# Last block of a hybrid mLSTM / chunk-MLP step: sample statistics moved, gate scans split, block end by token tile

## The chip, the cores and the metric

The kernel runs on one core of a Trainium2 chip. The metric is the device time of one execution in microseconds (us), as a median of several runs. Names of engines: PE is the matrix engine, DVE the vector engine, ACT the scalar engine, POOL the GpSimd engine, SP the queue that issues most loads.

## What is computed

One decoder layer for two groups with the same weights: a prompt of 2048 tokens and a group of 8 samples of one token each, which start from a stored state. Model width is 1024; there are 4 mLSTM heads and 4 chunk-MLP heads of width 128; the SwiGLU mixer has 2816 hidden columns. Everything is float32. The core of the reference, shortened:

```python
h = rmsnorm(x, g_norm1) * (1 + sc1) + sh1
q, k, vm, o, ig, fg, u, vs = split_cols(h @ w_in, IN_SIZES)
h_ml, C, n, m = mlstm_chunkwise(q, k, vm, i_pre, f_pre, C0, n0, m0)
h_ml = rmsnorm(h_ml, g_mlstm_head) * sigmoid(o)
vs = layernorm(gelu(vs), ln_v_g, ln_v_b)
h_cm = chunk_spatial_gate(gelu(u), vs, w_s, b_s)
x = x + gt1 * (concat([h_ml, h_cm]) @ w_out)
h2 = rmsnorm(x, g_norm2) * (1 + sc2) + sh2
a, bb = split(h2 @ w_gate_up)
x = x + gt2 * ((silu(a) * bb) @ w_down)
y = rmsnorm(x, g_final)
```

In `mlstm_chunkwise` the gates of a chunk of 128 tokens become b, the running sum of log_sigmoid(f), and a running maximum m_t; both scale the chunk's attention matrix and the state that goes to the next chunk. For one sample token these are a few numbers per head, and the state update is C_new = w_i C + w_g v k^T, with h = C_new q / den.

## The kernel before, in words

The prompt goes through in four blocks of 512 tokens (`NBLK`, `TT` = 4 token tiles of 128 each). The first block also works out the modulation, blocks 1 and 2 are a loop, and the last block also carries the samples and ends the program. Each engine has its own instruction list in program order; they meet at semaphores.

**Slabs.** Weights come in slabs of 512 KB. For slab s of a block, SP loads `raw` (two buffers), ACT rounds it into `w_hi` (`split_hi`, L842), DVE takes the difference into `w_lo` (`split_lo`, L1311), and PE makes three products per 128 rows (L1798 to L1800): hi times lo, lo times hi, hi times hi. `w_hi` and `w_lo` have two buffers as well, so slab s+2 can be split only when PE is done with slab s, and SP may load slab s only when slab s-2 has its low part.

**The order of the first part.** `PRE` and `MIX` are lists of steps that all engines go through. An integer s is the product of slab s of `w_in` on PE; at the same step ACT moves slab s out of its bank and splits slab s+2, and DVE makes the low part of slab s+2. Between them stand the prompt's gates: "R1" (`gate_sum`, L1329 to L1334), "R2" (`gate_log` on ACT: exp, then ln), "R3" (`gate_scans` on DVE, L1341 to L1357), "R4" (`gate_weights` on ACT) and "COL". R3 is four running sums (L1345), a difference, and then four times a running maximum (L1352) followed by one addition (L1354), with each waiting for the one before; two row operations end it, and they release `row_m`. SP waits for `row_m` ahead of slab 10's load.

**The samples** are put between these steps in the last block by the table `SAMPLES`, which PE, ACT and DVE all follow at the integer steps (DVE after its low part):

```python
SAMPLES = {2: ("SG",), 3: ("SW",), 4: ("SD",), 5: ("SC", "SV"), 6: ("C0",), 7: ("C1", "C2"), ...
```

SG is the samples' gates and two dot products, SW the stabiliser, SD the denominators, SC three copies out of PE's banks with one product that releases `wv_set` (L1260), SV the statistics of the samples' layernorm (six DVE steps, L1264 to L1269, after a gelu that ACT makes in SD, L811), and C0 to C7 update one sample's state each (three DVE steps, L1303 to L1306). On POOL `samples_state` (L633 to L640: three small products, then eight scalings of the stored states, after `wv_set`) comes first and `samples_mixing` (L583, L648 to L659: seven steps on 8 rows, after SV) second. `samples_mixing` needs the row `lnrow`, which SP loads at slab 8 (L469).

**The end of the last block.** The last slab's products fill four banks, a token tile each. For each tile DVE multiplies by the gate and adds to `x1` (`down_tiles`, L1477, L1479), ACT sums the squares of the tile's right half (L759; the left half's squares were summed during the slabs before). After the four tiles DVE copies the samples' product out (`s_ev`, L1628), PE turns it (`sample_turn`, L1832), DVE adds it (`sample_residual`), PE sums the squares (L1859), DVE takes the means (L1081, L1086), POOL the roots (L583), and DVE scales whole rows of `x1` by root and final gain (L1641, 1024 wide). SP stores each tile when its row is done (L559). The samples' result is turned by PE (L2162), moved out by ACT and DVE (L1033, L1659) and stored by ACT.

## Time and profile before

| | |
|---|---|
| median of 3 runs | 2534.2 us (2533.69 to 2534.28) |
| the profiled execution | 2534.6 us, of which the span of instructions is 2533.1 us |
| busy share of the span | PE 97%, DVE 47%, ACT 33%, POOL 7% |
| mean granted clock of PE | 0.989 of full speed |
| DMA | 280.13 MB, mean 111 GB/s |

All times inside the program are counted from the start of the span. A row of a timeline has the start, the duration, the engine, the line of the kernel and the operation with what it writes and reads; in brackets stands how long the engine sat idle before it and what ended that. The last block's first slab product begins at about 1844 us; the end of its last slab product is near 2514.8 us.

### The profile page before, as it was taken

The numbers are of one execution on the slowest core, as the hardware profiler recorded it, in microseconds if no ns is written. First come the engines' busy times: TensorE is split into PE (matmuls) and PEld (weight loads), VectorE is DVE, ScalarE is ACT, GpSimd is POOL, SyncE is SP. The second block draws the span as 40 slices with busy tenths as digits, with TensorE's granted clock in tenths as the row PEclk, the third lists the DMA queues.
The fourth block names the chain that finished last, engine by engine and source line by source line (L and its number), as shares of the span: only waits on it lengthen the run. The fifth ranks groups of instructions, "written<-read, shape, count | busy, mean of one in ns | idle before, by whom it ended". The sixth has DMA issues, their size and how long they took to land.

```text
span 2533.1 us, 32802 instructions
## 1 busy us (share of the span) xinstructions
PE 2454.7 (97%) x12328; PEld 1982.8 (78%) x12328; DVE 1202.8 (47%) x1741; ACT 846.2 (33%) x1149; POOL 182.8 (7%) x147
## 2 busy tenths in 40 slices
PE   5999999999999999999999999999988999999997
PEld 3688877888888888888888878888876877777775
DVE  4648545434347554444346654444367853333323
ACT  2343322233244243333244243333253323323211
POOL 0022000000003000000003100000033200000000
PEclk8999999999999999999999999999999999999998
DMA  7732365332342243332342333333354222222222
GB/s 274 260 100 80 116 191 173 109 94 96 114 115 70 89 125 91 99 100 89 100 137 71 98 112 95 98 93 97 99 185 134 79 67 77 81 83 83 87 88 76
DMA packets 361043, 280.13 MB, mean 111 GB/s; under 512 B 11288, under 2 KB 302652, under 8 KB 360919
## 3 DMA queue, kind: packets, MB, share of 16 engines
q1 hardware_dynamic: 333012, 228.91, 30.2%
q10 hardware_dynamic: 23956, 34.81, 4.0%
q0 software_dynamic: 3968, 14.95, 1.6%
q8 instruction: 71, 1.16, 0.2%
q14 instruction: 36, 0.29, 0.0%
HBM read 267.68 MB, written 10.96 MB: 110 GB/s over the span
## 4 chain that ended last, share of the span: by engine, by line
PE 85%; DVE 8%; DMA 2%; issue 2%; ACT 2%; POOL 0%; DVEq 0%; SPq 0%; POOLq 0%; ACTq 0%
PE banks L1798 18%; PE banks L1799 17%; PE banks L1800 17%; PE banks L1851 8%; PE banks L1853 8%; PE banks L1852 8%; DMA raw<-in_w_in_dram 2%; PE banks L1679 1%; PE banks L1812 1%; DMA stage<-in_w_ada_dram 1%; DVE w_lo L1311 1%; PE banks L1822 1%; ACT w_hi L842 1%; DVE x L1641 1%; PE banks L1997 1%
## 5 line engine op out<-in xcount | busy, mean ns | idle before, releaser
L1798 PE MATMUL banks<-hT_hi,w_lo 128*128 128x512 f32 x2176 | 864.3, 397 | 18.0 <-DVE w_lo L1311 15.7
L1799 PE MATMUL banks<-hT_lo,w_hi 128*128 128x512 f32 x2176 | 850.2, 391 | 0.0
L1800 PE MATMUL banks<-hT_hi,w_hi 128*128 128x512 f32 x2176 | 849.9, 391 | 0.0
L1311 DVE TENSOR_TENSOR w_lo<-raw,w_hi 128x1024 fp32r<-128x1024 f32 x392 | 480.2, 1225 | 618.7 <-ACT w_hi L842 607.8
L842 ACT ACTIVATE w_hi<-raw 128x1024 fp32r<-128x1024 f32 x392 | 412.6, 1053 | 475.1 <-PE banks L1853 441.4
L1798 PEld LDWEIGHTS banks<-hT_hi,w_lo 128*128 128x128 f32 x2176 | 409.8, 188 | 120.3 <-DVE w_lo L1311 17.1
L1800 PEld LDWEIGHTS banks<-hT_hi,w_hi 128*128 128x128 f32 x2176 | 409.5, 188 | 87.3
L1799 PEld LDWEIGHTS banks<-hT_lo,w_hi 128*128 128x128 f32 x2176 | 410.0, 188 | 81.1
L1851 PE MATMUL banks<-w_lo,act_hi 128*128 128x512 f32 x704 | 277.2, 394 | 0.0
L1853 PE MATMUL banks<-w_hi,act_hi 128*128 128x512 f32 x704 | 274.3, 390 | 0.0
L1852 PE MATMUL banks<-w_hi,act_lo 128*128 128x512 f32 x704 | 274.1, 389 | 0.0
L963 ACT ACTIVATE act_hi<-work 128x512 f32 (+1 forms) x88 | 55.6, 632 | 388.8 <-DVE work L1597 388.8
L1593 DVE TENSOR_TENSOR work<-work,banks 128x512 f32<-128x512 f32 x88 | 60.5, 687 | 263.3 <-ACT work L957 263.3
L1851 PEld LDWEIGHTS banks<-w_lo,act_hi 128*128 128x128 f32 x704 | 132.1, 188 | 35.4 <-issue 8.7
L1597 DVE TENSOR_TENSOR work<-work,banks 128x512 f32<-128x512 f32 x88 | 60.6, 688 | 207.2 <-PE banks L1800 207.2
L1853 PEld LDWEIGHTS banks<-w_hi,act_hi 128*128 128x128 f32 x704 | 132.2, 188 | 27.9
L1852 PEld LDWEIGHTS banks<-w_hi,act_lo 128*128 128x128 f32 x704 | 132.2, 188 | 26.5
L583 POOL TENSOR_TENSOR rrt<-msq,half 128x1 f32<-128x1 f32 (+1 forms) x27 | 18.0, 670 | 1563.0 <-DVE msq L1075 1168.9
L957 ACT ACTIVATE work<-banks 128x512 f32<-128x512 f32 x88 | 52.6, 598 | 183.0 <-PE banks L1800 182.6
L1851 PE MATMUL banks<-w_lo,mix_hi 128*128 128x512 f32 x256 | 100.9, 394 | 1.8 <-DVE w_lo L1311 1.2
L1852 PE MATMUL banks<-w_hi,mix_lo 128*128 128x512 f32 x256 | 99.7, 390 | 0.0
L1853 PE MATMUL banks<-w_hi,mix_hi 128*128 128x512 f32 x256 | 99.7, 389 | 0.0
(335 smaller groups left out, 1871.5 us busy)
## 6 DMA issues: line engine op xcount, KB each, us to landing
raw<-in_w_gate_up_dram SPq DMA_DIRECT2D x176, 512.0 KB, 3.7
raw<-in_w_in_dram SPq DMA_DIRECT2D x96, 512.0 KB, 3.8
raw<-in_w_down_dram SPq DMA_DIRECT2D x88, 512.0 KB, 3.8
ada_stage<-in_w_ada_dram ACTq DMA_DIRECT2D x8, 2048.0 KB
raw<-in_w_out_dram SPq DMA_DIRECT2D x32, 512.0 KB, 3.6
in_stage<-in_w_in_dram ACTq DMA_DIRECT2D x6, 2048.0 KB
stage<-in_w_ada_dram SPq DMA_DIRECT2D x4, 2048.0 KB
x_sb<-in_x_prompt_dram POOLq DMA_DIRECT2D x4, 2048.0 KB, 9.6
```

The lines of the kernel that those rows point to most:

```text
L842: act.activation(w_hi[:, s % 2], raw[:, s % 2], ACT.Copy).then_inc(hi_done.sem, 1)
L957: act.activation(work[:, 2], G[0][:, :], ACT.Sigmoid).then_inc(evac.sem, 1)
L963: act.activation(act_hi[:, bass.ds(pair_i * 2 + u, 1), :], work[:, 3:4, :], ACT.Copy)\
L1311: ve.tensor_tensor(w_lo[:, s % 2], raw[:, s % 2], w_hi[:, s % 2].bitcast(F32), ALU.subtract).then_inc(lo_done.sem, 1)
L1593: ve.tensor_tensor(work[:, 2], work[:, 2], G[0][:, :], ALU.mult).then_inc(silu_done.sem, 1)
L1597: ve.tensor_tensor(work[:, 3], work[:, 2], G[1][:, :], ALU.mult).then_inc(gated.sem, 1)
L1798: mm(out, w_lo[:, slot, k, :], rhs_hi[:, r, :], start=start and n == 0, stop=False)
L1799: mm(out, w_hi[:, slot, k, :], rhs_lo[:, r, :], start=False, stop=False)
L1800: ins = mm(out, w_hi[:, slot, k, :], rhs_hi[:, r, :], start=False, stop=stop and last)
L1851: mm(out, x_hi[:, k0 + k, t], lo[:, k, :], start=start and k == 0, stop=False)
L1852: mm(out, x_lo[:, k0 + k, t], hi[:, k, :], start=False, stop=False)
L1853: ins = mm(out, x_hi[:, k0 + k, t], hi[:, k, :], start=False, stop=stop and k == 1)
```

## The change

It moves SV from step 5 to step 2 and SC from step 5 to step 6; ACT's gelu for it goes from SD to SG. On POOL the samples' mixing goes ahead of the samples' state. SP loads `lnrow` at slab 6 instead of 8, and POOL uses the first row of `lnrow` as scratch instead of the samples' k. In the last block `gate_scans` has a middle: after the running sums and the difference, DVE makes the low part of slab 8 and then SC, and only then the running maxima; step 6 makes no low part any more.

At the end of the block `s_ev` is copied ahead of the last four tiles; the samples' turn and their sum of squares go between the tiles' products on PE; each tile's mean follows the tile after it. POOL multiplies the left halves of `x1` by the final gain as soon as their squares are summed, ACT scales a left half by the tile's root, and DVE only makes the right half (512 wide). SP waits for both.

```diff
-SAMPLES = {2: ("SG",), 3: ("SW",), 4: ("SD",), 5: ("SC", "SV"), 6: ("C0",), 7: ("C1", "C2"), 8: ("C3", "C4"),
+SAMPLES = {2: ("SG", "SV"), 3: ("SW",), 4: ("SD",), 6: ("SC", "C0"), 7: ("C1", "C2"), 8: ("C3", "C4"),
+SCANS_AT = 6
...
-                if s == 8:
+                if s == 6:
                     sp.wait_ge(sem("vo_ps"), 1)
...
             for i in range(TT):
                 sp.wait_ge(sem("y_row"), i + 1)
+                sp.wait_ge(y_left.sem, y_left.at(NBLK - 1, i + 1))
...
                 if last:
+                    samples_mixing()
                     samples_state()
-                    samples_mixing()
...
                 if last:
+                    pool.wait_ge(squared.sem, squared.at(blk, 3 * TT))
                     for i in range(TT):
-                        tile_root(blk, TT + i)
+                        pool.tensor_tensor(x1[:, i, 0:BLK], x1[:, i, 0:BLK], g_fin[:, 0:BLK], ALU.mult)\
+                            .then_inc(x1_gained.sem, 1)
+                    tile_root(blk, TT)
+                    tile_root(blk, TT + 1)
                     sample_root(2)
+                    tile_root(blk, TT + 2)
+                    tile_root(blk, TT + 3)
...
+                    def left_half(i):
+                        act.wait_ge(x1_gained.sem, x1_gained.at(blk, TT + i + 1))
+                        act.wait_ge(rs.sem, rs.at(blk, TT + i + 1))
+                        act.activation(x1[:, i, 0:BLK], x1[:, i, 0:BLK], ACT.Copy, scale=rrt[:, i:i + 1])\
+                            .then_inc(y_left.sem, 1)
...
                 link(ve.tensor_tensor(RT[0:H, :], rI, rb, ALU.subtract))
+                if last:
+                    split_lo(blk, SCANS_AT + 2)
+                    for_samples("SC")
...
+                if ending:
+                    ve.wait_ge(sem("s_read"), N_OUT + 2 * FT + N_DOWN)
+                    ve.tensor_copy(s_ev[:, :], SP_[:, :]).then_inc(sem("s_evict"), 1)
+                    left_mean(blk, 3 * TT)
...
+                    if i > 0:
+                        tile_mean(blk, 3 * TT, i - 1)
+                    if i == 1:
+                        sample_residual(N1, 2 + FT // 2, 3, s_x1[:, :, :], s_x2[:, :, :])
+                    if i == 2:
+                        sample_mean(2)
+
+            def final_rows(blk):
+
+                def right_half(i):
+                    ve.wait_ge(rs.sem, rs.at(blk, TT + i + 1))
+                    ve.scalar_tensor_tensor(out=x1[:, i, BLK:D], in0=x1[:, i, BLK:D], scalar=rrt[:, i:i + 1],
+                                            in1=g_fin[:, BLK:D], op0=ALU.mult, op1=ALU.mult).then_inc(sem("y_row"), 1)
+
+                right_half(0)
+                tile_mean(blk, 3 * TT, TT - 1)
+                sample_scaled(2, s_x2[:, :, :])
+                ve.tensor_tensor(s_h32[:, :, :], s_t[:, :, :], each_head(prmT[:, PR_GF:PR_GF + KT], NB), ALU.mult)\
+                    .then_inc(sem("s_ready"), 1)
+                for i in range(1, TT):
+                    right_half(i)
...
+                        if last and n == N_DOWN - 1 and i == 1:
+                            sample_turn(N1, 2 + FT // 2)
+                        if last and n == N_DOWN - 1 and i == 2:
+                            sample_sum(N2)
```

DVE, last block, from the low part of slab 7 (first row) into the scans, before. `colq` is SC's, `proj`, `dots` and `sm_*` are SV's, `rows` and `RT` are the prompt's gate rows:

```order
L1311 TENSOR_TENSOR w_lo<-raw,w_hi 128x1024
L1255 COPY colq<-banks 128x128
L1257 COPY colq<-banks 128x64
L1260 TENSOR_TENSOR colq<-colq 128x32
L1264 TENSOR_REDUCE sm_mean<-proj 8x4
L1265 TENSOR_SCALAR sm_den<-sm_mean 8x4
L1266 TENSOR_TENSOR proj<-proj,sm_den 8x512
L1267 TENSOR_TENSOR dots<-proj 8x512
L1268 TENSOR_REDUCE sm_mean<-dots 8x4
L1269 TENSOR_SCALAR sm_var<-sm_mean 8x4
L1341 SCALAR_TENSOR_TENSOR rows<-rows 4x512
L1345 SCALAR_TENSOR_TENSOR rows<-onerow,rows 4x128 x4
```

The same place with the change (the code's lines are moved by some 18; the row with x4 is the running sums, those with `mst` the running maxima, and both kinds of scan are listed as SCALAR_TENSOR_TENSOR):

```order
L1329 TENSOR_TENSOR w_lo<-raw,w_hi 128x1024
L1359 SCALAR_TENSOR_TENSOR rows<-rows 4x512
L1363 SCALAR_TENSOR_TENSOR rows<-onerow,rows 4x128 x4
L1366 TENSOR_TENSOR RT<-rows 4x512
L1329 TENSOR_TENSOR w_lo<-raw,w_hi 128x1024
L1273 COPY colq<-banks 128x128
L1275 COPY colq<-banks 128x64
L1278 TENSOR_TENSOR colq<-colq 128x32
L1373 SCALAR_TENSOR_TENSOR rows<-last_row,mst,RT 4x128
L1375 TENSOR_TENSOR mst<-rows 4x1
```

The samples' statistics have left the place, and the low part of slab 8 and SC stand between the running sums and the running maxima. Behind the last row come three more pairs of a maximum and an addition, the two row operations that release `row_m`, C0's three steps, and only then the low part of slab 9.

POOL, last block, all of the samples' steps of this part, before (`sm_quant`, `n_177` and `C_150` are the state's, `sm_rv`, `lnrow`, `sm_w`, `sm_bs` the mixing's; the last row is the prompt's):

```order
L633 TENSOR_TENSOR proj<-proj,sm_quant 8x512
L634 TENSOR_TENSOR n_177<-n_177,sm_quant 8x512
L636 TENSOR_TENSOR n_177<-n_177,proj 8x512
L640 TENSOR_TENSOR C_150<-C_150,colq 128x512 x8
L583 TENSOR_TENSOR sm_rv<-sm_var,half 8x4
L648 TENSOR_TENSOR proj<-proj,sm_rv 8x512
L651 TENSOR_TENSOR proj<-proj,lnrow 8x512
L653 TENSOR_TENSOR proj<-proj,lnrow 8x512
L655 TENSOR_TENSOR proj<-proj,sm_w_199 8x512
L657 TENSOR_TENSOR proj<-proj,sm_bs_200 8x512
L659 TENSOR_TENSOR proj<-proj 8x512
L617 TENSOR_TENSOR decay<-decay,mask 128x512
```

And with the change:

```order
L586 TENSOR_TENSOR sm_rv<-sm_var,half 8x4
L651 TENSOR_TENSOR proj<-proj,sm_rv 8x512
L654 TENSOR_TENSOR proj<-proj,lnrow 8x512
L656 TENSOR_TENSOR proj<-proj,lnrow 8x512
L658 TENSOR_TENSOR proj<-proj,sm_w_199 8x512
L660 TENSOR_TENSOR lnrow<-proj,sm_bs_200 8x512
L662 TENSOR_TENSOR proj<-lnrow,proj 8x512
L636 TENSOR_TENSOR proj<-proj,sm_quant 8x512
L637 TENSOR_TENSOR n_177<-n_177,sm_quant 8x512
L639 TENSOR_TENSOR n_177<-n_177,proj 8x512
L643 TENSOR_TENSOR C_150<-C_150,colq 128x512 x8
L620 TENSOR_TENSOR decay<-decay,mask 128x512
```

The seven steps of the mixing now run before the state's three products and eight scalings.

DVE, end of the last block, from the fourth tile's addition on, before (`s_*` are the samples', `msq` the tiles' means):

```order
L1479 TENSOR_TENSOR x_56<-x_56,work 128x512
L1628 COPY s_ev<-banks 128x512
L1502 TENSOR_TENSOR s_t_131<-banks,modS 128x64
L1503 TENSOR_TENSOR s_x_128<-s_t_131,s_x_127 128x64
L1504 TENSOR_TENSOR s_sq<-s_x_128 128x64
L1509 TENSOR_REDUCE s_sum<-banks 128x8
L1511 TENSOR_SCALAR s_ms<-s_sum 128x8
L1081 TENSOR_SCALAR left_ms<-ssum 128x4
L1086 SCALAR_TENSOR_TENSOR msq<-ssum,left_ms 128x1 x4
L1641 SCALAR_TENSOR_TENSOR x_56<-x_56,rrt,g_fin 128x1024 x2
L1517 TENSOR_TENSOR s_t<-s_x_128,s_r 128x64
```

And with the change, from the second tile's addition to the fourth tile's:

```order
L1504 TENSOR_TENSOR x_56<-x_56,work 128x512
L1104 SCALAR_TENSOR_TENSOR msq<-ssum,left_ms 128x1
L1550 TENSOR_TENSOR s_t_131<-banks,modS 128x64
L1551 TENSOR_TENSOR s_x_128<-s_t_131,s_x_127 128x64
L1552 TENSOR_TENSOR s_sq<-s_x_128 128x64
L1502 TENSOR_TENSOR work<-banks,work 128x512
L1504 TENSOR_TENSOR x_56<-x_56,work 128x512
L1104 SCALAR_TENSOR_TENSOR msq<-ssum,left_ms 128x1
L1557 TENSOR_REDUCE s_sum<-banks 128x8
L1559 TENSOR_SCALAR s_ms<-s_sum 128x8
L1502 TENSOR_TENSOR work<-banks,work 128x512
L1504 TENSOR_TENSOR x_56<-x_56,work 128x512
```

The copy `s_ev` and `left_ms` have gone ahead of the tiles, the samples' steps stand between them, and the rows of 1024 have become halves of 512.

## Rows read from the trace of the kernel before

**Rows 1.** Waits of PE, whole program: who for whom, us in total, times, longest.
```profile
PE banks L1798 <- DVE w_lo L1311: 15.7, 6, 13.7
```

**Rows 2.** Windows: length, busy us (instructions) of PE, PEld, DVE, ACT, POOL; clock, DMA.
```profile
1900.00:1904.00 4.00, 0.00 (x0) 0.00 (x0) 3.89 (x4) 0.00 (x0) 3.77 (x4) 0.50 0.00 0
...
1908.00:1910.00 2.00, 1.97 (x5) 1.59 (x6) 1.97 (x4) 1.94 (x6) 0.00 (x0) 0.50 0.45 70
```

**Rows 3.** Timeline of PE: first products of slabs 7, 8, 9; what follows.
```profile
1888.18 0.48 PE L1798 MATMUL banks<-hT_hi,w_lo 128*128 128x512 f32 x1
...
1908.03 0.80 PE L1798 MATMUL banks<-hT_hi,w_lo 128*128 128x512 f32 x1 [13.68 <-DVE w_lo L1311]
...
1915.65 0.39 PE L1798 MATMUL banks<-hT_hi,w_lo 128*128 128x512 f32 x1
...
1921.10 0.60 PE L1927 MATMUL banks<-ident,RT 128*128 128x128 f32 x4
```

**Rows 4.** Timeline of DVE, slabs 5 to 8 of the last block.
```profile
1872.81 1.23 DVE L1311 TENSOR_TENSOR w_lo<-raw,w_hi 128x1024 fp32r<-128x1024 f32 x1 [3.92 <-ACT w_hi L842]
...
1878.79 1.24 DVE L1238 SCALAR_TENSOR_TENSOR sm_quant<-sm_qk,sm_quant 8x4 f32<-8x4 f32 x1
...
1884.87 1.23 DVE L1311 TENSOR_TENSOR w_lo<-raw,w_hi 128x1024 fp32r<-128x1024 f32 x1 [3.50 <-ACT w_hi L842]
...
1897.81 0.47 DVE L1352 TENSOR_TENSOR_SCAN rows<-last_row,mst,RT 4x128 f32<-4x128 f32 x1
...
1899.17 1.56 DVE L1352 TENSOR_TENSOR_SCAN rows<-last_row,mst,RT 4x128 f32<-4x128 f32 x1
```

**Rows 5.** One line's instructions, all four blocks: ns min/median/max, first and last start.
```profile
L1345 DVE TENSOR_TENSOR_SCAN rows<-onerow,rows x16: 385/388/1194, 114.1 to 1895.9; 4x128 f32<-4x128 f32 x16
L1352 DVE TENSOR_TENSOR_SCAN rows<-last_row,mst,RT x16: 471/472/1559, 116.3 to 1904.1; 4x128 f32<-4x128 f32 x16
```

**Rows 6.** Timeline of POOL, last block: scalings, one step of the mixing, the first mask.
```profile
1886.92 9.87 POOL L640 TENSOR_TENSOR C<-C,colq 128x512 f32<-128x512 f32 x8 [6.91 <-DVE colq L1260]
...
1899.20 1.25 POOL L651 TENSOR_TENSOR proj<-proj,lnrow 8x512 f32<-8x512 f32 x1
...
1915.66 1.29 POOL L617 TENSOR_TENSOR decay<-decay,mask 128x512 f32<-128x512 f32 x1 [10.32 <-DMA decay<-max_rows]
```

**Rows 7.** Timeline of ACT: high part of slab 5, table load for gelu.
```profile
1871.64 1.06 ACT L842 ACTIVATE w_hi<-raw 128x1024 fp32r<-128x1024 f32 x1 [3.26 <-DMA raw<-in_w_in_dram]
...
1876.70 1.28 ACT L811 ACT_TABLE_LOAD   x1
```

**Rows 8.** Loads of `raw` issued from 1862 to 1880 us: issue to landing.
```profile
DMA to landing us min/median/max: 3.8/4.7/9.7
```

**Rows 9.** Timeline of DVE, end of the program.
```profile
2510.78 0.69 DVE L1477 TENSOR_TENSOR work<-banks,work 128x512 f32<-128x512 f32 x1 [6.08 <-PE banks L1853]
...
2516.52 0.69 DVE L1479 TENSOR_TENSOR x<-x,work 128x512 f32<-128x512 f32 x1
...
2524.30 2.48 DVE L1641 SCALAR_TENSOR_TENSOR x<-x,rrt,g_fin 128x1024 f32<-128x1024 f32 x2 [2.02 <-POOL rrt L583]
...
2527.09 2.47 DVE L1641 SCALAR_TENSOR_TENSOR x<-x,rrt,g_fin 128x1024 f32<-128x1024 f32 x2
```

**Rows 10.** Timeline of PE, end of the program: last slab product, turn, sum of squares.
```profile
2514.39 0.39 PE L1853 MATMUL banks<-w_hi,act_hi 128*128 128x512 f32 x1
2517.87 1.95 PE L1832 MATMUL banks<-ssel,s_ev 128*128 128x8 f32 x16 [3.09 <-DVE s_ev L1628]
2520.65 0.69 PE L1859 MATMUL banks<-s_sq,onerow 128*128 128x64 f32 x2 [0.83 <-DVE s_sq L1504]
```

**Rows 11.** Timeline of POOL and ACT, end: roots; squares of the fourth tile.
```profile
2522.16 2.11 POOL L583 TENSOR_TENSOR rrt<-msq,half 128x1 f32<-128x1 f32 x4 [140.90 <-DVE msq L1086]
...
2517.25 0.63 ACT L759 ACTIVATE junk<-x 128x512 bf16<-128x512 f32 x1 [0.91 <-DVE x L1479]
```

**Rows 12.** DMA issues from 2520 us on: KB each, median us from issue to landing.
```profile
out_dram<-x SPq DMA_DIRECT2D x4, 512.0 KB, 2.6
```

More of the change, by code:

```diff
@@ L375, in hybrid_step @@
         hm_done = signal("hm_done", TT)
+        y_left, x1_gained = right_scaled, hm_done
         hmtr = signal("hmtr", H)
@@ L656, in samples_mixing @@
                 pool.wait_ge(done, 4)
-                pool.tensor_tensor(by_head(k8), by_head(q8), each_head(sm["bs0"][:, :]), ALU.add).then_inc(done, 1)
+                pool.tensor_tensor(by_head(lnrow[:, 0, :]), by_head(q8), each_head(sm["bs0"][:, :]), ALU.add).then_inc(done, 1)
                 pool.wait_ge(done, 5)
-                pool.tensor_tensor(q8, k8, u8, ALU.mult).then_inc(done, 1)
+                pool.tensor_tensor(q8, lnrow[:, 0, :], u8, ALU.mult).then_inc(done, 1)
             def pool_block(blk, last):
                 if last:
+                    samples_mixing()
                     samples_state()
-                    samples_mixing()
                 mask_decay(blk, 0)
@@ L798, in for_samples @@
                 if step == "SG":
+                    act.wait_ge(sem("proj_in"), 48)
+                    act.activation(proj[:, GATE0:], proj[:, GATE0:], ACT.Gelu_apprx_tanh)\
+                        .then_inc(sem("gelus"), 1)
                     act.wait_ge(sem("nAs"), 1)
@@ L809, in for_samples @@
                     fetch("small_out", m_sample[0], sm["m"][:, :])
-                elif step == "SD":
-                    act.activation(proj[:, GATE0:], proj[:, GATE0:], ACT.Gelu_apprx_tanh)\
-                        .then_inc(sem("gelus"), 1)
                 elif step == "SC":
@@ L1007, in act_block @@
                         squares(blk, 1, x1, BLK, D, 1, rows=(i,))
+                        if i > 0:
+                            left_half(i - 1)
+                    left_half(TT - 1)
                 else:
@@ L1335, in gate_sum, with gate_scans @@
                     .then_inc(row_n.sem, 1)
-            def gate_scans(blk):
+            def gate_scans(blk, last=False):
                 rI, rF, rlf, rL, rb, rM, rbm = (rows[0:H, i, :] for i in (0, 1, 2, 4, 5, 6, 7))
@@ L1480, in down_tiles @@
                         .then_inc(zadd.sem, 1)
-            handlers = {"R1": gate_sum, "R3": gate_scans, "COL": gate_columns, "WD": decays,
+                    if not ending:
+                        continue
+                    if i > 0:
+                        tile_mean(blk, 3 * TT, i - 1)
[15 more added lines that the diff above has]
+                    right_half(i)
+            handlers = {"R1": gate_sum, "COL": gate_columns, "WD": decays,
                         "VST": vs_stats, "CMS": spatial, "ML": finish_heads}
@@ L1535, in ve_block @@
                     if isinstance(step, int):
-                        if step + 2 <= N_WIN:
+                        if step + 2 <= N_WIN and not (last and step == SCANS_AT):
                             split_lo(blk, step + 2)
@@ L1553, in ve_block @@
                         for piece in SAMPLES.get(step, ()) if last else ():
-                            for_samples(piece)
+                            if piece != "SC":
+                                for_samples(piece)
+                    elif step == "R3":
+                        gate_scans(blk, last)
                     elif step in handlers:
@@ L1625, in ve_block @@
                     if n % DOWN_Q == 0:
-                        down_tiles(blk, n // DOWN_Q - 1)
+                        down_tiles(blk, n // DOWN_Q - 1, last and n == N_DOWN)
                 if last:
-                    ve.tensor_copy(s_ev[:, :], SP_[:, :]).then_inc(sem("s_evict"), 1)
-                    sample_residual(N1, 2 + FT // 2, 3, s_x1[:, :, :], s_x2[:, :, :])
-                    sample_mean(2)
-                else:
-                    split_lo(blk, NSLAB + 1)
-                if last:
-                    left_mean(blk, 3 * TT)
-                    for i in range(TT):
-                        tile_mean(blk, 3 * TT, i)
-                    ve.wait_ge(rs.sem, rs.at(blk, 2 * TT))
-                else:
-                    mean_square(blk, 2)
+                    final_rows(blk)
+                    return
+                split_lo(blk, NSLAB + 1)
+                mean_square(blk, 2)
                 for i in range(TT):
@@ L1642, in ve_block @@
                                                   in1=g_fin[:, :], op0=ALU.mult, op1=ALU.mult)
-                    if last:
-                        ins.then_inc(sem("y_row"), 1)
-                    if last and i == 1:
-                        sample_scaled(2, s_x2[:, :, :])
-                        ve.tensor_tensor(s_h32[:, :, :], s_t[:, :, :],
-                                         each_head(prmT[:, PR_GF:PR_GF + KT], NB), ALU.mult)\
-                            .then_inc(sem("s_ready"), 1)
-                if not last:
-                    ins.then_inc(y_done.sem, 1)
-                    round_off(BLK_CHAIN)
+                ins.then_inc(y_done.sem, 1)
+                round_off(BLK_CHAIN)
             ve_block(0, False, first=True)
@@ L2151, in pe_block @@
                         norm_out(blk, range(c, c + 4))
-                if last:
-                    sample_turn(N1, 2 + FT // 2)
-                    sample_sum(N2)
             pe_block(0, False, first=True)
```

2 lines of the change are left out of this document (1 added, 1 removed).

## Prediction

> **What bounds the kernel now.** I read the waits of PE first, then PE's timeline around the longest one, then what DVE, POOL and ACT did meanwhile, and last the end of the program. PE is busy for 97% of the span, so time can only come out of its few gaps and out of the ends. One gap stands out: of 15.7 us that slab products waited for a low part, 13.7 is a single wait [rows 1], ahead of slab 8 of the last block, where PE is idle until 1908.03 [rows 3]. It costs more than itself: PE's clock is at half in it and still after it [rows 2], so that slab 8 takes 7.6 us from its first product to slab 9's, where slab 9 takes 5.45 [rows 3]: 2.2 more. ACT and the loads are not the reason. DVE makes the low part of slab 7 at 1884.87 and then SC, the samples' statistics SV and all of R3 before it turns to slab 8 [rows 4]. And it does these slowly: a scan of 0.39 or 0.47 us takes up to 1.19 or 1.56 in this place alone [rows 5], because POOL runs its scalings and its mixing there [rows 6]. At the end of the program, 2514.8 to 2533.1, PE has only small work; DVE, PE, POOL and DVE again follow one another [rows 9 to 11].
>
> **The front, part by part.** Times are on the clock of the trace before.
>
> SV moves to step 2. Its three row operations of about 0.69 [rows 9] and three small steps make some 3.2 us, and DVE sat idle for 3.92 there, until slab 5's high part came [rows 4]. ACT's gelu goes with it: a table load of 1.28 and about 1.06 of work into an idle time of 3.26, which slab 5's load ends [rows 7]. Cost: nothing for both; were that load earlier, slab 5 would be late by up to 3.2. At the old place ACT loses the gelu, its table load and the reload of exp's table, 3.6 in sum, so slab 7's high part is not late although the gates before it are.
>
> `lnrow`'s two loads go between those of slabs 6 and 7 on SP. The slowest slab load there took 9.7 us [rows 8]; that is slab 6's, and I take `lnrow` to land just behind it, near 1876. SP waits for nothing new: the transposes it asks for are long done.
>
> POOL now runs the mixing's seven steps and the state's three from about 1872 to 1886, about 1.0 to 1.25 each [rows 6], beside SW, R1 and SD on DVE, where before it had three steps. The price of a meeting is in the rows: an 8x4 step took 1.24 [rows 4], and a scan of 0.47 took 1.56 [rows 4, 5]; so a DVE step with both inputs in SBUF waits for about one POOL step of 1.1. I count two such waits more ahead of slab 6's low part, which ended at 1878.8 where SD's first step starts [rows 4] and now ends near 1880.9. In SD I count four more, by POOL's last four steps. SD then ends at 1887.2, and slab 7's low part at 1888.4 instead of 1886.1 [rows 4]. Ends: with no more meetings it ends at 1884.3, with one for each of SD's steps at 1890. PE starts slab 7 at 1888.5, where it was 1888.18 [rows 3].
>
> **The rule against the row.** The scan that started at 1899.17 was ahead of POOL's step of 1899.20 and still took 1.56 instead of 0.47 [rows 4 to 6]; so where DVE's steps wait for each other, POOL gets in between them. The Trainium skill, page "SBUF — State Buffer", section "Who interferes with whom", says that the one that issues first holds the shared ports for its whole instruction and the other is blocked. Read strictly, SD's closely spaced steps would stay ahead of POOL, and the sum would be some 4 us better; this is the first rival below, and that row speaks against it.
>
> The first half of R3 meets an idle POOL, which waits for SC: four running sums of 0.39 [rows 5] and two row operations of 0.69 make 3.0, to 1891.4. Slab 8's low part, 1.23, to 1892.6; SC 0.8 (1886.1 to 1886.92, where it released POOL [rows 4, 6]), to 1893.4. PE does slab 7 and four transposes until 1894.4, so **slab 8 waits for nothing**, and ends at 1899.9.
>
> The second half stands fully beside the eight scalings, which SC releases. Before it ran from 1897.81 [rows 4] to about 1906.8 (slab 8's low part, 1.23, follows and PE starts at 1908.03): 9.0 beside seven POOL steps. Eight scalings take 9.87 [rows 6]; I take 9.5, to 1902.9. Ends: 4.0 on free ports (four scans of 0.47, four small steps, two of 0.69), which only an idle POOL would give, and 11. Then C0, three steps of 0.69, to 1905.0, and slab 9's low part to 1906.2. So PE waits again, one slab later: from 1899.9 to 1906.2, 6.3 us. Before, the half clock was there from 6 us of idling on at the latest [rows 2, 3], so I charge slab 9 the 2.2 that slab 8 paid; the other end is nothing.
>
> Slab 9 starts at 1906.2 instead of 1915.65 [rows 3], 9.45 earlier, less 2.2: **the front gains 7.3**. What follows must keep up. `row_m` comes at 1902.9, only 3.3 ahead of slab 9 where it was 8.8. ACT's nine exponentials then end near 1906.9, slab 10's high part near 1909 and its low part, behind C1 and C2, near 1911; slab 9 ends at 1913.9. SP is held at `row_m` ahead of slab 10's load, 3.8 us at best [rows 8]: in place at 1907, one us before ACT wants it.
>
> **The end, part by part.** DVE's copy `s_ev` and the left means go into the 6.08 that it waits ahead of the first tile [rows 9]: free, and if that cover were gone, 0.9. On PE the turn, 1.95, and the sum, 0.69 [rows 10], with their starts, push the last slab product from 2514.39 to about 2517.4. Tile 4's pair on DVE ends at 2519.5, not at 2517.2 [rows 9]: 2.3 lost. Behind it now stand only that tile's squares (0.63 and a read [rows 11]), one mean and one root (2.11 for four [rows 11]), to 2521.2; DVE has by then made the first right half, at half of 1.24 [rows 9], and the samples' two steps, and makes the other three to 2523.1. ACT's left halves of about 0.6 end at 2521.9, ahead of DVE. POOL's four gains, 1.29 each as a 128x512 step [rows 6], run while the last slab is multiplied, before the first addition; if they are late, each tile waits up to 1.3. Before, the last row was done at 2529.56 (2527.09 and 2.47 [rows 9]) and the span ended 3.5 later, 2.6 of it the store [rows 12]. Three stores now leave within 1.3 us, not 1.2 apart; I add 0.9 for that: 2527.5. **The end gains 5.6**; bounds 3.5 (late gains, or a chain of stores) and 6.5 (stores that overlap).
>
> **Sum.** 7.3 + 5.6 = 12.9 off the profiled execution's 2534.6, which is 0.4 above the median of the runs: **2521.7**. Its own range, from SD's ends and those of the end, is 2519 to 2524.
>
> **The rivals.**
> 1. *DVE keeps the ports.* SD ends some 4 us earlier, slab 9 starts near 1902.9 after a wait of 5.0; 3 to 4 more, and up to 2.2 if the clock stays up: 2516 to 2518.5, say 2517.5. For it: SD's steps are tiny; against it: the row of 1899.17.
> 2. *A load takes the wait's place.* Slab 10's load starts only at `row_m`, and slab 11's stands behind four loads for the masks. If slab 10's takes 9.7 as slab 6's did, it is 1.4 late, and slab 11's some 2: 2525. For it: the small margin; against it: DMA moved nothing at 1900 to 1904 [rows 2], so the queues are empty then.
> 3. *The stall only moves.* If meetings cost the chain from SW to slab 9's low part another 7 us, PE waits as long as before, ahead of slab 9, and only the end gains: 2529.0. Against it: POOL has 18 steps in all, and I have charged most of them.
> 4. *Slower.* POOL's list is now one chain behind `lnrow`: five steps of the mixing, three of the state, the first scaling, some 10 us, then C0 and the low part, 3.3, to slab 9. If `lnrow` lands later than 1908, the program is slower than before; at 1914 or later by over 0.2%, say 2541. It would need some 48 us for two loads of 16 KB, and the slowest slab load took 9.7 [rows 8].
>
> **The numbers.** Chances: forecast 0.60, rivals 0.22, 0.10, 0.05, 0.03. The range, 2515.5 to 2526.5, takes in the forecast and the first two rivals. A change of 0.2% (5.1 us) is about what the measurement can tell from none. Faster by more than that: 0.60 + 0.22 + 0.10 = 0.92; within it 0.05, the third rival; slower 0.03.
>
> **What would show it.** No PE wait at slab 8 and one of about 6 us at slab 9, with half clock in it; SV before slab 5's low part with no POOL beside it; SD's steps of over 1 us between 1881 and 1887; scans of the running sums at 0.39 and those of the maxima still at 1.1 to 1.6 beside the scalings; the last right half some 6 us earlier and the last store 2.6 to 4 behind it. The forecast is wrong if PE waits at slabs 6, 7, 10 or 11 for over 1 us each, if C0 waits for POOL, or if the last tile's addition ends later than 2520 less the front's gain.

## The result, and the profile after

The changed kernel takes 2519.1 us (median of four runs, 2517.8 to 2520.4) where the kernel before takes 2534.2 beside it: ratio 0.994, 95% interval 0.9925 to 0.9956, so 15.1 us less. Run once more with a later experiment it gave 2519.2 (ratio 0.9937, 0.9925 to 0.9950). The forecast was 2521.7, within 2515.5 to 2526.5. The profiled execution took 2520.4, 1.3 above the median of its four; its span is 2518.8, 14.3 shorter than before. Three executions in all the rounds, at 3080 to 7035 us, lie far above the others of their kernels and are left out of the medians and ranges given here.

The waits of PE in the whole program, as [rows 1] (who for whom, us in total, times, longest):

```profile
PE banks L1833 <- DVE w_lo L1329: 9.1, 7, 6.8
...
PE banks L1969 <- DVE col L1382: 2.4, 1, 2.4
```

The long wait for a low part is halved, from 13.7 to 6.8. The wait for `col`, ahead of slab 11, is new in this size. The kernel before had:

```profile
PE banks L1934 <- DVE col L1361: 1.4, 1, 1.4
```

So had the second trace of the changed kernel (`changed_again`, experiment 12): 1.4.

PE's timeline, as [rows 3]: first products of slabs 7, 8 and 9, the transposes for `col`, and the product behind `col`.

```profile
1886.25 0.47 PE L1833 MATMUL banks<-hT_hi,w_lo 128*128 128x512 f32 x1
...
1892.16 0.48 PE L1833 MATMUL banks<-hT_hi,w_lo 128*128 128x512 f32 x1
...
1904.66 0.80 PE L1833 MATMUL banks<-hT_hi,w_lo 128*128 128x512 f32 x1 [6.77 <-DVE w_lo L1329]
...
1911.66 0.60 PE L1962 MATMUL banks<-ident,RT 128*128 128x128 f32 x4
...
1920.16 0.40 PE L1969 MATMUL banks<-col,last_row 128*128 128x16 f32 x2 [2.41 <-DVE col L1382]
```

Slab 8 waits for nothing; the one wait stands ahead of slab 9. The transposes for `col` start 9.4 earlier than in [rows 3], 0.4 of which this execution had already gained ahead of the changed place. Slab 9 takes 7.0 to them, 1.55 more than the 5.45 of a slab at full clock.

Windows, columns as in [rows 2]: the clock in the wait, in slab 9, and behind the wait for `col`.

```profile
1902.00:1904.00 2.00, 0.00 (x0) 0.00 (x0) 1.97 (x4) 1.95 (x5) 0.00 (x0) 0.50 0.43 85
...
1906.00:1908.00 2.00, 2.00 (x6) 1.54 (x6) 1.97 (x4) 2.00 (x5) 0.00 (x0) 0.57 1.09 318
...
1922.00:1924.00 2.00, 2.00 (x6) 1.52 (x5) 1.86 (x7) 0.00 (x0) 0.00 (x0) 0.50 0.70 150
```

The third window is a second stretch at half clock, seven products long, behind the wait for `col`. It costs some 1.6, and the second trace of the same kernel has none of it.

Such stretches differ from one execution to the next. Half clock in slab 9 costs 1.55 here, 1.9 in the second trace, and 2.8 and 3.0 in two experiments with the same front (`front_alone` and `half_stores`). In the second of these, slab 9's first product and the transposes for `col`:

```profile
1904.50 0.79 PE L1836 MATMUL banks<-hT_hi,w_lo 128*128 128x512 f32 x1 [6.77 <-DVE w_lo L1332]
...
1912.96 0.60 PE L1965 MATMUL banks<-ident,RT 128*128 128x128 f32 x4
```

And the trace before has such a stretch where this one has none, far behind the changed place, at two groups of products for the samples. Before, and then here:

```profile
2096.83 1.94 PE L1812 MATMUL banks<-raw,s_hp 128*32 128x128 f32 x32
...
2105.03 0.64 PE L1812 MATMUL banks<-raw,s_hp 128*32 128x128 f32 x16
```

```profile
2090.03 1.08 PE L1847 MATMUL banks<-raw,s_hp 128*32 128x128 f32 x32
...
2096.91 0.65 PE L1847 MATMUL banks<-raw,s_hp 128*32 128x128 f32 x16
```

From the first group to the second it is 8.2 before and 6.9 here, a difference of 1.3 that the change did not make: six of the fourteen traces have the stretch, among them `front_alone` with the new front, and `end_alone` with the old front has none. The spread of the runs, 2.6, may well be made of such stretches; only traces show them, not the times.

DVE, as [rows 4, 5]:

```profile
1868.51 0.68 DVE L1282 TENSOR_REDUCE sm_mean<-proj 8x4 f32<-8x512 f32 x1
...
1872.30 1.23 DVE L1329 TENSOR_TENSOR w_lo<-raw,w_hi 128x1024 fp32r<-128x1024 f32 x1 [0.60 <-ACT w_hi L851]
...
1880.73 1.00 DVE L1260 TENSOR_TENSOR sm_den<-sm_den,sm_quant 8x4 f32<-8x4 f32 x1
...
1884.36 1.21 DVE L1329 TENSOR_TENSOR w_lo<-raw,w_hi 128x1024 fp32r<-128x1024 f32 x1
1885.49 1.52 DVE L1359 SCALAR_TENSOR_TENSOR rows<-rows 4x512 f32<-4x512 f32 x1
1887.04 2.35 DVE L1363 TENSOR_TENSOR_SCAN rows<-onerow,rows 4x128 f32<-4x128 f32 x4
...
1893.32 1.24 DVE L1373 TENSOR_TENSOR_SCAN rows<-last_row,mst,RT 4x128 f32<-4x128 f32 x1
...
1903.39 1.22 DVE L1329 TENSOR_TENSOR w_lo<-raw,w_hi 128x1024 fp32r<-128x1024 f32 x1
```

SV (from L1282) fills what was idle ahead of slab 5's low part: 0.60 is left of 3.92. The second product of SD takes 1.00 where it took 0.15 before; two more steps of SD grow like it, while its first, at 0.99, was slow before already (1.24 in [rows 4]). The first half of R3 is not free: its first step takes 1.52 and its four sums 2.35, where four of 0.385 were forecast.

ACT, as [rows 7]: gelu at its new place, and the high part of slab 5.

```profile
1865.55 1.06 ACT L809 ACTIVATE proj<-proj 8x1024 f32<-8x1024 f32 x1
...
1871.21 1.06 ACT L851 ACTIVATE w_hi<-raw 128x1024 fp32r<-128x1024 f32 x1 [1.10 <-DMA raw<-in_w_in_dram]
```

ACT still waits 1.10 for slab 5's load there, so gelu costs nothing.

POOL, as [rows 6]: the first step that needs `lnrow`, a step of the mixing, two of the state, and the last six of the eight scalings (the first starts at 1892.18).

```profile
1875.37 1.29 POOL L654 TENSOR_TENSOR proj<-proj,lnrow 8x512 f32<-8x512 f32 x1 [0.94 <-DMA lnrow<-in_ln_v_b_dram]
...
1878.10 2.50 POOL L658 TENSOR_TENSOR proj<-proj,sm_w 8x512 f32<-8x512 f32 x1
...
1884.04 2.42 POOL L637 TENSOR_TENSOR n<-n,sm_quant 8x512 f32<-8x512 f32 x1
1886.54 1.62 POOL L639 TENSOR_TENSOR n<-n,proj 8x512 f32<-8x512 f32 x1
...
1894.24 6.43 POOL L643 TENSOR_TENSOR C<-C,colq 128x512 f32<-128x512 f32 x6
```

The loads of `lnrow`, placed among those of [rows 8], land by 1875.4 (1876 in the forecast) and cost POOL 0.94. Where the engines meet, POOL's steps grow too: the steps of 2.50 and 2.42, each beside a low part, took 1.03 before. So the state ends at 1888.2, inside the first half of R3.

The end: DVE, as [rows 9], with the `s_ev` copy, the pair of tile 4, the first and the other three right halves.

```profile
2501.12 0.69 DVE L1497 COPY s_ev<-banks 128x512 f32<-128x512 f32 x1 [4.53 <-PE banks L1857]
...
2508.97 0.69 DVE L1502 TENSOR_TENSOR work<-banks,work 128x512 f32<-128x512 f32 x1
2509.81 0.69 DVE L1504 TENSOR_TENSOR x<-x,work 128x512 f32<-128x512 f32 x1
...
2511.79 2.07 DVE L1519 SCALAR_TENSOR_TENSOR x<-x,rrt,g_fin 128x512 f32<-128x512 f32 x3
```

PE's turn and sum, as [rows 10]; then POOL's last two roots, as [rows 11]:

```profile
2503.77 1.85 PE L1867 MATMUL banks<-ssel,s_ev 128*128 128x8 f32 x16
2506.93 0.33 PE L1894 MATMUL banks<-s_sq,onerow 128*128 128x64 f32 x2
```

```profile
2510.94 1.21 POOL L586 TENSOR_TENSOR rrt<-msq,half 128x1 f32<-128x1 f32 x2
```

The stores, as [rows 12]: two windows, whose last two columns are the busy share of the 16 DMA engines and GB/s; then the four stores' time from issue to landing.

```profile
2512.00:2513.00 1.00, 1.00 (x6) 0.59 (x7) 1.00 (x2) 1.00 (x3) 0.15 (x1) 0.50 0.93 385
...
2515.00:2516.00 1.00, 0.00 (x0) 0.00 (x0) 0.00 (x0) 0.00 (x0) 0.00 (x0) 0.50 1.04 426
```

```profile
DMA to landing us min/median/max: 2.6/2.9/4.5
```

The last row is done at 2513.86 and the span ends 4.9 later, not 3.5: its store lands 4.5 after its issue because the 16 DMA engines are busy from 2512 to 2517.5, at about 400 GB/s, with the three stores ahead of it (experiment 10 tests this). The Trainium skill, page "DMA: Bandwidth & Descriptors", section "Specifications", gives 435 GB/s as the ceiling on the SBUF side; the four windows from 2512 to 2516 come close, at 385 to 426.

### The profile page after: what moved, and what is told of

Its sections match the earlier page's. It is cut to its first block, busy times and chain, and to the rows that moved or that the text cites. A ratio compares the mean times of both kernels' runs of the same rounds, so it can differ in the third digit from the quotient of the medians.

```text
span 2518.8 us, 32818 instructions
## 1 busy us (share of the span) xinstructions
PE 2453.3 (97%) x12328; PEld 1982.3 (79%) x12328; DVE 1202.7 (48%) x1741; ACT 847.6 (34%) x1152; POOL 188.4 (7%) x151
## 4 chain that ended last, share of the span: by engine, by line
PE 85%; DVE 8%; issue 2%; DMA 2%; ACT 2%; SPq 0%; ACTq 0%; POOL 0%; DVEq 0%
PE banks L1833 17%; PE banks L1834 17%; PE banks L1835 17%; PE banks L1886 8%; PE banks L1888 8%; PE banks L1887 8%; DMA raw<-in_w_in_dram 1%; PE banks L1714 1%; DVE w_lo L1329 1%; PE banks L1847 1%; DMA stage<-in_w_ada_dram 1%; PE banks L1857 1%; PE banks L2032 1%; PE banks L2010 1%; DVE CN L1402 1%
```

## The experiments

The theory after the result: the front and the end add up; in the front, DVE is what PE waits for, without a gap from 1890 to 1924, and POOL's steps beside it cost it time wherever they stand. So a wait of PE goes only if DVE's work gets less, or if its order puts what PE wants first. The main rivals: the split or the early SV alone does it; the scans are slow in themselves; the wait at slab 9 is a price by itself. All edits are of the changed kernel; gains are against the kernel before in the same rounds. Differences from the changed kernel are between medians of different rounds, in which the kernel before itself moves by up to 1.0.

**1 and 2. One part at a time.** `front_alone` has the old end, `end_alone` the old front.

```diff
-                        down_tiles(blk, n // DOWN_Q - 1, last and n == N_DOWN)
+                        down_tiles(blk, n // DOWN_Q - 1)
...
```

> Edit: the changed front (SV early, scans in two halves, POOL's mixing ahead of its state), with the old end of the block. Theory (front and end add up): on the changed kernel's trace the last slab is 8.1 us earlier than before, 0.4 of it already there ahead of the changed place, so the front alone gives 7.7: 2534.2 - 7.7 = 2526.5, with a PE wait of about 6.8 at slab 9. Rival (the parts are not independent, the end's gain hangs on the front): 2528 or more, or below 2525.

```diff
-SAMPLES = {2: ("SG", "SV"), 3: ("SW",), 4: ("SD",), 6: ("SC", "C0"), ...
+SAMPLES = {2: ("SG",), 3: ("SW",), 4: ("SD",), 5: ("SC", "SV"), 6: ("C0",), ...
...
```

> Edit: the old front, with the changed end of the block. Theory (front and end add up): from the first half's last addition to the end of the span the changed kernel needs about 6.1 us less, so 2534.2 - 6.1 = 2528.1, with the 13.7 us wait at slab 8 still there. Rival (the new end only works because the front leaves the engines earlier): 2530 or more.

Measured: the front alone 2524.2 (ratio 0.9961, 0.9948 to 0.9974), 10.3 less than before; the end alone 2527.6 (0.9975, 0.9966 to 0.9984), 6.9 less. The end came as the theory had it. The front did not: 2524.2 is below 2525, which I had given to the rival, that the parts hang on each other. Their sum, 17.2, is 2 above the whole; by the intervals (6.6 to 13.2 and 4.1 to 8.6) it cannot be told from the whole, so independence is neither refuted nor shown by the times.

The traces put the front lower. PE's turn of the samples at 2086.94 in the trace before lies behind the front's waits and ahead of the stretch at 2097. It comes 6.4 earlier in the changed kernel's first trace, 8.8 in its second, 7.7 in `front_alone` and 7.5 in `half_stores`, if each trace's offset ahead of the changed place (0.2 to 0.8) is taken out. These four differ mostly by half clock: in slab 9, and behind the wait for `col` in the first alone. Behind the stretch at 2097 the first two gain 1.3 more, because they lack it. `front_alone`'s trace is of the slowest of its five executions (2527.3), with 2.8 of half clock in slab 9 and the stretch at 2097; an execution with 1.55 and without the stretch would be 2.6 faster. That would give most of the 3.1 to its median, but no trace of a faster execution shows it.

**3. Without the split.** `whole_scans`:

```diff
-                if last:
-                    split_lo(blk, SCANS_AT + 2)
-                    for_samples("SC")
...
+                        if last:
+                            for_samples("SC")
                         gate_scans(blk, last)
```

> Edit of the changed kernel: the split alone undone; SC ahead of R3, R3 in one piece, slab 8's low part behind it; SV and POOL's mixing stay early. Theory (PE can use the time only if slab 8 can run while the second half of the scans does): R3 ends near 1900.6, slab 8's low part near 1901.8, a PE wait of about 9.6 at slab 8 in place of 6.8 at slab 9, slab 9 starts near 1908.8 instead of 1904.7, of which the shorter wait for col gives back 1 to 2: 2521.5 to 2523. Rival (DVE's work up to slab 9's low part is what counts, its order does not): 2519.1, as the changed kernel.

Measured: 2522.4 (ratio 0.9952, 0.9940 to 0.9965), 3.3 more than the changed kernel and inside the theory's range; its fastest run, 2521.5, is slower than the slowest of the changed kernel, 2520.4. The page's waits of PE:

```profile
PE banks L1832 <- DVE w_lo L1329: 12.3, 6, 10.7
...
PE banks L1968 <- DVE col L1379: 1.4, 1, 1.4
```

DVE has the same work up to slab 9's low part, but PE sits idle for 10.7 ahead of slab 8: the order counts.

**4. Without the early samples.** `sv_back` keeps the split and puts SV, gelu, the loads of `lnrow` and POOL's mixing where they were:

```diff
+SAMPLES = {2: ("SG",), 3: ("SW",), 4: ("SD",), 5: ("SV",), 6: ("SC", "C0"), ...
...
                 if last:
+                    samples_state()
                     samples_mixing()
-                    samples_state()
...
```

> Edit of the changed kernel: SV, ACT's gelu, the loads of lnrow and POOL's mixing at their old places; the scans stay in two halves around slab 8's low part and SC. Theory (SV was on DVE's chain there and free where it is now): 3.2 us, and the meetings with POOL's state, come back ahead of R3; slab 8 waits for its low part for some 2 us and slab 9 for about 8, the time is 2522 to 2524. Rival (the split alone does it, SV's place is worth nothing): 2519.1.

Measured: 2527.1 (ratio 0.9972, 0.9961 to 0.9983), 8 more, where the theory had said 3 to 5. Slab 8 waits 0.5, where I had said 2, slab 9 for 8.3, and `col` 4.8. DVE's timeline shows what I had left out:

```profile
1904.86 2.06 DVE L1329 TENSOR_TENSOR w_lo<-raw,w_hi 128x1024 fp32r<-128x1024 f32 x1
1906.84 1.76 DVE L1321 TENSOR_TENSOR q_all<-C,q_all 128x512 f32<-128x512 f32 x1
...
1913.11 2.30 DVE L1329 TENSOR_TENSOR w_lo<-raw,w_hi 128x1024 fp32r<-128x1024 f32 x1
```

The mixing now stands beside the low parts and the C steps. They take 2.06 to 2.30 instead of 1.22 and 1.76 instead of 0.68: 5.4 over seven steps, just where DVE has no gap; 1.1 of it, beside POOL's mask, the changed kernel pays too (a C step of 1.79). So, by the trace, moving the mixing to where DVE was waiting for ACT anyway (3.50 ahead of slab 7's low part, [rows 4]) is worth more than moving SV's 3.2; no run moves one without the other.

**5. The price of POOL.** `late_scalings` holds the eight scalings until the scans are done:

```diff
                 pool.wait_ge(sem("wv_set"), 1)
+                pool.wait_ge(row_m.sem, row_m.at(NBLK - 1, 1))
                 for b in range(NB):
```

> Edit of the changed kernel: POOL holds its eight scalings until row_m, so that the second half of the scans has no POOL beside it. Theory (POOL beside DVE makes the scans slow, at some 0.66 us a scaling, and the price follows the scalings wherever DVE has work): the second half takes about 4.3 us instead of 9.6 (scans of 0.47, row operations of 0.68), row_m comes near 1896.3; C0 then waits for the first scaling and meets the next ones, slab 9's low part ends between 1900.5 and 1903, the PE wait there is 3 to 5 us instead of 6.8, the later C steps are slow beside the other scalings, the wait for col stays or grows, and the time is 2517 to 2519.5. Rival (the scans are slow in themselves here, because they wait for one another): second half still 9 us or more, C0 later still, 2522 or more. Second rival (only the scans suffer, the C steps do not): 2514 or less.

Measured: 2517.8 (2517.7 to 2522.3; ratio 0.9941, 0.9928 to 0.9954), inside the theory's range and no different from the changed kernel. DVE's timeline, from an execution of 2521.7:

```profile
1892.56 0.47 DVE L1374 TENSOR_TENSOR_SCAN rows<-last_row,mst,RT 4x128 f32<-4x128 f32 x1
1893.06 0.15 DVE L1376 TENSOR_TENSOR mst<-rows 4x1 f32<-4x1 f32 x1
...
1900.47 2.06 DVE L1330 TENSOR_TENSOR w_lo<-raw,w_hi 128x1024 fp32r<-128x1024 f32 x1
1902.46 1.53 DVE L1322 TENSOR_TENSOR q_all<-C,q_all 128x512 f32<-128x512 f32 x1
1904.03 0.69 DVE L1323 TENSOR_REDUCE colq<-q_all 128x4 f32<-128x512 f32 x1
```

The scans are fast by themselves: the second half takes 3.8 (1892.56 to 1896.32) instead of 9.6, so eight scalings had cost it 5.8. Moved, they take 3.8 from slab 9's low part and the C steps with two inputs (2.06 instead of 1.22, and 1.45 to 1.53 instead of 0.67), and C0 waits 1.3 for the first of them. They pay too: the eight take 11.3 instead of 8.5. The reduction between them stays at 0.69, beside POOL or not. PE waits 4.1 at slab 9, and 3.7 instead of 2.4 for `col`.

**6. C0 behind slab 9's low part.** `c0_behind`:

```diff
-                            if piece != "SC":
+                            if piece not in ("SC", "C0"):
...
+                        if last and step == 7:
+                            for_samples("C0")
```

> Edit of the changed kernel: DVE's C0 (three steps, 2.0 us) goes behind slab 9's low part. Theory (DVE is busy without a gap from 1890 to 1924, so what it owes by the copy of col sets the time): the wait at slab 9 falls from 6.8 to about 4.8, the wait for col grows from 2.4 to about 4.4, and the time stays at 2519.1, at most 0.8 less if the half clock is shorter. Rival (the wait at slab 9 alone is what it costs): 2.0 faster than the changed kernel, 2517.1.

Measured: 2518.0 (2517.2 to 2521.6; ratio 0.9940, 0.9927 to 0.9953), 1.1 less than the changed kernel: between the theory (at most 0.8) and the rival (2.0), and by the time alone neither can be excluded. The trace is for the theory. The wait at slab 9 falls by 2.0, to 4.8, but the product behind `col` starts only 0.6 earlier than in the changed kernel's first trace and no earlier than in its second (offsets taken out). The wait for `col` grows only to 2.8, because a C step meets POOL's mask for 0.4 here and not for 1.1.

**7. The copy of `col` first.** `col_first` adds to that:

```diff
-           9: ("C5", "C6"), 10: ("C7", "SQ"), 11: ("ST", "SN"), 12: ("SX",)}
+           10: ("C5", "C6"), 11: ("C7", "SQ", "ST", "SN"), 12: ("SX",)}
...
```

> Edit of the changed kernel: C0 behind slab 9's low part, and the copy of col ahead of C5 and C6 (these one step later, C7 with the samples' last row operations too). Theory (what DVE owes by the copy of col and by the samples' squares sets the time): the wait for col, 2.4 to 2.8, goes; slab 11 starts some 2.5 earlier, and the squares at 1923 are then just in time: 2516.0 to 2517.5. Rival (the wait only moves on to the samples' sum or to slab 12): 2518.7, as with C0 behind alone.

Measured: 2520.6 (ratio 0.9948, 0.9935 to 0.9961): a miss, and the rival, with more than its price. The page's waits:

```profile
PE banks L1835 <- DVE w_lo L1329: 6.9, 7, 4.8
...
PE banks L1824 <- DVE colq L1300: 5.5, 1, 5.5
```

The wait for `col` is gone, and one of 5.5 for the samples' squares (L1300) has come. DVE had stood idle for 2.9 ahead of slab 12's low part, which waits for ACT, with C5 queued behind it.

**8. C5 and C6 straight behind the copy.** `c56_behind_col` closes that gap: C0 behind slab 9's low part, and

```diff
+                        if last and step == "COL":
+                            for_samples("C5")
+                            for_samples("C6")
...
```

> Edit of the changed kernel: C0 behind slab 9's low part, and C5 and C6 directly behind the copy of col, ahead of slab 12's low part (with C5 and C6 one step later DVE had stood idle for 2.9 ahead of that low part, and the samples' squares had come 4 us late). Theory (DVE owes a fixed sum of work by the samples' squares; only its order against PE's waits is free): no wait for col, DVE without a gap, squares at 1923.4, a PE wait of about 0.8 for them: 2516 to 2517.5. Rival (the wait moves on to the squares in full): 2518.7.

Measured: 2516.1 (2514.4 to 2517.3; ratio 0.9926, 0.9912 to 0.9939), in the theory's range and 3.0 under the changed kernel. The page's waits of PE: no `col`, and 1.6 for the squares.

```profile
PE banks L1838 <- DVE w_lo L1329: 7.6, 7, 4.9
...
PE banks L1827 <- DVE colq L1300: 1.6, 1, 1.6
```

**9. Four scalings on ACT.** `scaled_by_act`, on top of that:

```diff
-                for b in range(NB):
+                for b in range(NB // 2):
...
+                        for h in range(H):
+                            ins = act.activation(C0[:, b, h, :], C0[:, b, h, :], ACT.Copy, scale=colq[:, 13, h, b:b + 1])
...
```

> Edit: C5 and C6 behind col as in the kernel beside it, and ACT makes the last four of the eight scalings (four 128x128 activations each, 1.27 us) in place of POOL. Theory (each scaling of POOL's beside DVE costs DVE some 0.66; ACT's cost it nothing): the second half of the scans takes about 7 us instead of 9.6, the wait at slab 9 falls from 4.8 to about 2.2, the squares come at 1920.8: 2513.5 to 2516. Rival (ACT becomes the bound in slabs 8 to 11, with 6.6 us of work in a slab of 5.5): 2517 or more, with waits for high parts.

Measured: 2516.8 (2514.0 to 2518.6; ratio 0.9927, 0.9914 to 0.9941): no gain that can be told from the kernel without it, and a median between the theory's 2516 and the rival's 2517. The second half takes 6.7 and slab 9 waits 1.9, as the theory said, but DVE then waits 0.6 for ACT ahead of C7, PE 1.3 for ACT's evictions and 2.4 for the squares. So ACT takes the bound over in part, as the rival said, though not by a high part.

**10. Half-row stores.** `half_stores`, the changed kernel with eight stores, each as soon as its half is done:

```diff
-            for i in range(TT):
...
-                sp.dma_start(y_last[:, i, :], x1[:, i, :]).then_inc(sem("y_rows_out"), 16)
+            for left, i in ((1, 0), (1, 1), (0, 0), (1, 2), (0, 1), (1, 3), (0, 2), (0, 3)):
...
+                sp.dma_start(y_last[:, i, cols], x1[:, i, cols]).then_inc(sem("y_rows_out"), 16)
```

> Edit of the changed kernel: the last four row tiles are stored as eight halves, each as soon as it is done. Theory (the end is set by the DMA engines, busy from 2512.0 to 2517.5 at about 400 GB/s with 2.1 MB, because no row is whole before 2511.2): the first left halves leave at 2507.4 and 2510.2, the transfers end near 2515.7, and the last store lands 1.2 to 2.0 earlier: 2517.1 to 2517.9. Rival (the last store takes what it takes because of its own start and completion, 2.6 as before and the rest by chance): 2519.1, or later by the four more issues.

Measured: 2518.8 (2516.8 to 2521.7; ratio 0.9941, 0.9928 to 0.9954), too little to tell by the times. In one trace the last right half ends at 2513.8, as in the changed kernel, and the span 0.9 earlier, at 2517.9. That the end moves while the last half does not speaks for the theory. It is less than the 1.2 to 2.0 expected, because SP issues the last four stores 0.5 apart, the last 0.5 after its half was done.

**11 and 12. Both, beside the changed kernel.** `both_best` is 8 and 10 together; `changed_again` has no edit.

> Edit: the order of DVE's C pieces (C0 behind slab 9's low part, C5 and C6 behind col) and the eight half-row stores, in one kernel. Theory (they stand in different places and add up): the order gave 2516.1 against the changed kernel's 2519.1, the half stores 0.9 of the span in one trace: 2515.2, and faster than the changed kernel beside it by 3 to 4.5. Rival (the half stores were worth nothing but chance): 2516.1.

> The changed kernel once more, unedited, on the chip and in the rounds of the kernel beside it. If its runs so far are typical: 2519.1, between 2517.5 and 2521, the spread from whether a second stretch of half clock falls behind the wait for col.

Measured: 2515.2 (2511.7 to 2516.4; ratio 0.9919, 0.9906 to 0.9933) and 2519.2 (2517.8 to 2519.9). The version beats both kernels: 4.0 under the changed one in the same rounds, with no run of one inside the range of the other. Between 8 and this kernel the medians differ by 0.9, as much as the half stores gained in their trace; but they are from different rounds and their intervals overlap, so the rival, that the half stores are worth nothing, is not excluded by the times.

## Why the prediction was right, and where its sizes were off

**The front, 7.3 forecast.** Its steps happened as written: SV hidden, `lnrow` landed in time (POOL used it at 1875.4), no wait at slab 8, one of 6.8 at slab 9 where 6.3 was forecast, the second half of the scans 9.6 (9.5). Four traces give 6.4 to 8.8, 7.6 on average; only the medians of `front_alone`, 10.3, say more. In the first trace, where the front gives 6.4, four differences nearly cancel: slab 9 starts 1.2 earlier than forecast, its half clock costs 0.65 less, the wait for `col` 1.0 more, and the stretch of half clock behind it 1.6. So the sum is closer than its terms, and that is luck.
- *The meetings.* I counted two more ahead of slab 6's low part, four in SD and none in the first half of R3, at 1.1 each. The trace has two (0.8 each), some three and a half in SD (0.6 to 1.0), and two in the first half of R3 (0.85 and 1.0), because POOL's own steps were stretched to 2.5 and its state ended at 1888.2, not 1886. That is some 7 in all, but about 1.4 of it, most of this in SD's first step, was in the trace before already; I had charged 6.6 on top. On the clock of the trace before (0.4 added), SD ended at 1884.8 (forecast 1887.2) and slab 8's low part at 1891.7 (1892.6). The early end that I gave SD, 1884.3, does not come out of the rows: 1880.9 and the 2.6 that SD took before make 1883.5. And SV has four row operations, not three; the 3.2 that I gave it is what it took.
- *The half clock.* I charged slab 9 the 2.2 that slab 8 had paid. It paid 1.55 in this trace, and 1.9, 2.8 and 3.0 in the three others with this front: the charge was right, the single trace was not typical.
- *What follows.* "What follows must keep up" looked at loads and high parts, and these did. It did not look at the copy of `col`, which stands behind C5 and C6 on DVE: in the first trace 1.0 lost there, and a stretch of half clock behind it. By my own list, a wait of over 1 at slab 11 was a sign of being wrong; this one is 2.4, though 1.4 of it was there before.

**The end, 5.6 forecast, 6.2 in the trace.** To compare, I add the 8.1 by which the last slab is earlier (6.4 by the front, 0.4 ahead of it, 1.3 by the stretch at 2097). PE's last product is at 2516.4 (forecast 2517.4): the turn costs 1.7, but the sum, 0.33 long, almost nothing. Tile 4's pair ends at 2518.6 (2519.5), the last root at 2520.3 (2521.2), the last right half at 2522.0 (2523.1). From there the span needs 4.9, not 4.4. I gave the stores 0.9 for leaving closer together; it is 1.4, and by the windows and experiment 10 the DMA engines' throughput sets it. No row stood behind the 0.9. Front and end together are 12.6 in this trace, with 12.9 forecast; the medians give 15.1 against the 12.5 that 2521.7 meant for them.

**The rivals.** The first, DVE keeping the ports, gave 2517.5, nearer to the result than its mechanism deserves: three steps of SD did take 0.99 to 1.15 instead of 0.15, and experiment 5 shows a scan of 0.47 against 1.24 with nothing changed but POOL. The rule of the Trainium skill (page "SBUF — State Buffer", section "Who interferes with whom"), read as I had read it for a chain of short steps, is not what these rows show: POOL gets one step in between two dependent ones of DVE. Where the same page of the Trainium skill says that a reduction never contends, the rows agree, at 0.69 either way. A load that takes the wait's place, and POOL's chain behind `lnrow`, did not come: no wait of PE at slabs 10 or 11 names a load. The third, that the stall only moves, came by half, as the forecast itself had it: 6.8 of 13.7.

## What to carry to other kernels

When one engine is busy without a gap between two waits of another, removing one of these waits moves most of it to the next thing that this engine owes (experiments 6 and 7); follow the queue to its next gap before counting the gain, and reorder so that what is waited for stands first without opening a gap ahead of it (experiment 8). Work on POOL is not free just because POOL is idle: put it where DVE waits for somebody else, not where DVE is the chain. Before you explain a difference of 1 to 3 us between two traces, follow one product after another through both: here stretches of half clock that came and went made as much, at places that nobody had changed.

## What was not expected of the hardware

- One scaling of POOL costs DVE some 0.5 to 0.7, whether it meets scans (5.8 for eight in the second half of R3) or a low part and C steps (3.8 for the seven of experiment 5 that had DVE beside them). DVE costs POOL too: steps of 1.03 take 2.42 and 2.50 beside a low part.
- A row operation with one input, 4x512 in SBUF, is held up too: L1377 takes 1.24 beside POOL and 0.42 without it (experiment 5), where reductions are not.
- In one and the same kernel, or the same front, PE's half clock after a wait of 6.8 to 7.3 costs 1.55 to 3.0. Behind a wait of 2.4 for `col` it fell to half; behind one of 2.8 in `c0_behind` it did not.
- Stores of whole rows that become ready within 2.6 us leave as one block: 2.1 MB take 5.5 us at about 400 GB/s, and the last one lands after 4.5 where [rows 12] have 2.6.
